# Half of the second feed-forward matrix by seven block products for eight, with the feed-forward stage ordered anew

## The reference

```python
f = rms_norm(h, g_ffn_pre[l])
f = jnp.square(jax.nn.relu(f @ w_ff1[l])) @ w_ff2[l]
h = h + rms_norm(f, g_ffn_post[l])
```

## Time and profile before

| | |
|---|---|
| median of 3 runs | 2151.79 us (2151.78 to 2152.73) |
| span of the profiled execution | 2150.6 us, 1.2 us under the median |
| PE busy | 2125.1 us (99%) |
| DVE busy | 1361.9 us (63%) |
| ACT busy | 1106.1 us (51%) |
| POOL busy | 156.2 us (7%), all in slices 21 to 25 of 40 |
| DMA | 395.17 MB, mean 184 GB/s |

### The profile page before, as it was taken

One profiled execution on the slowest core, in us unless ns is written; L12 is line 12 of the kernel. 1 busy time (PEld: TensorE's weight loads), 2 busy tenths in 40 slices (PEclk: granted clock), 3 DMA queues, 4 the chain that ended last, 5 costly groups with the idle time before them and its releaser, 6 DMA issues. The chain is left out here.

```text
span 2150.6 us, 29240 instructions
## 1 busy us (share of the span) xinstructions
PE 2125.1 (99%) x11602; PEld 1841.8 (86%) x11602; DVE 1361.9 (63%) x1979; ACT 1106.1 (51%) x1541; POOL 156.2 (7%) x78
## 2 busy tenths in 40 slices
PE   8999999999999999999999999999999999999998
PEld 7888888888988888888888888888888888888886
DVE  5554568875577558876578678766555555555555
ACT  4444554454464555555455455656435534544543
POOL 0000000000000000000007873000000000000000
PEclk9999999999999999999999999999999999999999
DMA  8666545655576655655656654646666666666664
GB/s 278 196 189 187 165 138 174 179 172 186 185 214 186 178 148 159 174 167 176 191 180 198 193 178 151 215 136 206 193 193 190 189 193 193 189 194 190 192 190 145
DMA packets 325031, 395.17 MB, mean 184 GB/s; under 512 B 20848, under 2 KB 252912, under 8 KB 324128
## 3 DMA queue, kind: packets, MB, share of 16 engines
q1 hardware_dynamic: 323104, 383.21, 59.0%
q0 software_dynamic: 1792, 10.10, 1.2%
HBM read 391.16 MB, written 2.10 MB: 183 GB/s over the span
## 5 line engine op out<-in xcount | busy, mean ns | idle before, releaser
L490 DVE TENSOR_TENSOR low<-raw,high 128x1024 fp32r<-128x1024 f32 (+2 forms) x672 | 809.9, 1209 | 639.0 <-ACT high L934 635.3
L934 ACT ACTIVATE high<-raw 128x1024 fp32r<-128x1024 f32 (+2 forms) x732 | 763.0, 1046 | 775.8 <-PE acc L682 201.7
L682 PE MATMUL acc<-xhl,high 128*128 128x512 f32 x3198 | 766.4, 391 | 0.0
L682 PEld LDWEIGHTS acc<-xhl,high 128*128 128x128 f32 x3198 | 587.0, 188 | 113.8 <-issue 0.7
L699 PE MATMUL acc<-xhl,low 128*128 128x256 f32 x3200 | 436.9, 286 | 1.9 <-DVE xhl L1792 1.4
L699 PEld LDWEIGHTS acc<-xhl,low 128*128 128x128 f32 x3200 | 414.4, 191 | 18.1 <-DVE xhl L1792 1.8
L686 PE MATMUL acc<-high,yhl 128*128 128x512 f32 (+1 forms) x1036 | 380.1, 373 | 2.2 <-DVE work L1718 1.6
L687 PE MATMUL acc<-high,yhl 128*128 128x512 f32 (+1 forms) x1036 | 378.8, 372 | 0.0
L702 PE MATMUL acc<-low,yhl 128*128 128x512 f32 (+1 forms) x1036 | 241.9, 374 | 0.2
L686 PEld LDWEIGHTS acc<-high,yhl 128*128 128x128 f32 x1036 | 195.2, 188 | 36.8 <-DVE work L1718 2.0
L687 PEld LDWEIGHTS acc<-high,yhl 128*128 128x128 f32 x1036 | 195.2, 188 | 33.8
(11 more groups left out here) (228 smaller groups left out, 1286.9 us busy)
## 6 DMA issues: line engine op xcount, KB each, us to landing
raw<-in_w_in SPq DMA_DIRECT2D x328, 512.0 KB, 3.7
raw<-in_w_ff SPq DMA_DIRECT2D x256, 512.0 KB, 3.9
raw<-in_w_out SPq DMA_DIRECT2D x91, 512.0 KB, 4.3
raw<-in_w_mem_kv SPq DMA_DIRECT2D x32, 512.0 KB, 5.0
raw<-in_w_in SPq DMA_DIRECT2D x16, 256.0 KB, 2.7
raw<-in_w_out SPq DMA_DIRECT2D x10, 256.0 KB, 2.8
x_nat<-in_mem SPq DMA_DIRECT2D x4, 512.0 KB, 7.8
x_nat<-in_x POOLq DMA_DIRECT2D x4, 512.0 KB, 6.4
```

The source lines that it names most:

```text
L490: eng.tensor_tensor(part(low, g), part(raw, g), part(high, g).bitcast(F32), ALU.subtract).then_inc(ready, 1)
L682: ins = pe.matmul(acc[:, 2 * (c.acc % 2) + s, :], wh[:, t, at], vhl, start=first, stop=last)
L934: act.activation(part(high, g), part(raw, g), ACT.Copy).then_inc(high_ready, 1)
```

## The change

The first matrix is now computed in 64 tiles of 128 hidden features (two blocks each, rows of 128 columns, 512 bytes of a row of the weights in one piece), apart from the first four, which stay in the old interleaved chunks. All tiles after tile 4 use one PSUM bank (`obank`). Two tiles are a pair: 256 hidden features.

The second matrix is cut in two. For the first 28 pairs, its columns 0 to 1023 are taken as 2 x 2 blocks of 128 hidden features by 512 columns, and the hidden features as 2 x 2 blocks of 128 rows by 128 features; Strassen's scheme (in Winograd's form) takes seven products of sums of blocks instead of eight. Such a *group* is 14 matmuls of 512 columns with high weight parts (`group_high`), one or two tiles, then 7 with low weight parts (`group_low`). The seven sums stay in seven PSUM banks over a run of four groups. After each run come eight *piece* blocks, the same four pairs by columns 1024 to 2047 in the plain way, and the products are added to SBUF. The last four pairs take plain pieces for all columns.

So ACT and DVE gain work: sums of weight blocks (`group_sums`), seven units of 512 columns to split instead of four, sums of hidden blocks (`pair_sums`) with eight units of 128 to split instead of four, copies of each tile out of its bank (`tile_copy`). The row norm is folded into the end (`epsv`), so the scaled sums `sq3` go. `low_part` writes the low part over the raw block, and a slot of `raw` is free only when PE has used it. The order on each engine is written out again; with p0 to p7 I call the eight piece blocks of a run. The accumulators in SBUF are set to zero by POOL.

The core of the diff (of PE, then ACT, DVE, SP):

```diff
+def ff_order():
+    yield from (("tile", 4), ("tile", 5))
+    for j in range(GROUPS):
+        yield ("high", j)
+        if BESIDE[j][0] is not None:
+            yield ("tile", BESIDE[j][0])
+        yield ("low", j)
+        yield ("tile", BESIDE[j][1])
+        if j % 4 == 3:
+            yield from (("piece", j // 4, n, i) for n in (2, 3) for i in range(4))
+    for i in range(2):
+        for n in range(2):
+            yield ("piece", RUNS, n, i)
+            yield ("tile", 60 + 2 * i + n)
+    yield from (("piece", RUNS, n, i) for i in (2, 3) for n in range(2))
+    yield from (("piece", RUNS, n, i) for n in (2, 3) for i in range(4))
...
             eng.wait_ge(high_ready, g + 1)
-            eng.tensor_tensor(part(low, g), part(raw, g), part(high, g).bitcast(F32), ALU.subtract).then_inc(ready, 1)
+            out = part(rawr if g >= FF1 else low, g)
...
+        def tile_bank(n):
+            return bank_of[1] if n == TILES_AHEAD else obank[:, :]
...
+            def feature_tile(n):
+                if n > TILES_AHEAD + 1:
+                    pe.wait_ge(tile_out, n - TILES_AHEAD)
+                    if n - 12 in range(0, 56, 8):
+                        pe.wait_ge(piece_out, 4 * ((n - 12) // 8) + 3)
...
+            def group_high(j):
+                pe.wait_ge(pair_ready, j + 1)
+                pe.wait_ge(split_high, 3 * j + 3)
+                for p, unit, n in PRODUCTS:
...
+            def group_low(j):
+                pe.wait_ge(split_low, 3 * j + 3)
+                for p, unit, n in PRODUCTS:
+                    ins = pe.matmul(bank_of[p], rows_of(0, j, n), bset_r[:, j % 2, unit, :], start=False, stop=j % 4 == 3)
+                ins.then_inc(group_used, 1)
...
+            def piece(e, n, i, rows=(0, 1)):
+                g, pair = by["f2", e, n].blocks[i], 4 * e + i
+                wh, wl = part(high, g), part(rawr, g)
+                banks = last_banks[n]
+                pe.wait_ge(pair_ready, pair + 1)
...
+            def x_squares(c):
+                act.wait_ge(norm_ready, norms(2, 2 * c + 1))
+                squares(x[:, :, CW * c:CW * c + CW], c, junk=ff_junk)
...
+            def tile_copy(n):
+                act.wait_ge(block_used, last_of(("g1", n)))
+                if n >= TILES_AHEAD + 2:
+                    act.wait_ge(pair_sq, n // 2)
+                act.activation(tcopy[:, n % 2, :], tile_bank(n), ACT.Copy).then_inc(tile_out, 1)
+            def relu_of(pair):
+                if pair < 2:
+                    act.wait_ge(folded, flip_no(by["f1", 0, pair]) + 1)
+                    v = cross
+                else:
+                    act.wait_ge(pair_fold, pair - 1)
+                    v = tcopy[:, :, 0:S]
+                act.activation(v, v, ACT.Relu).then_inc(pair_relu, 1)
+                act.wait_ge(pair_relu, pair + 1)
+                if pair:
+                    act.wait_ge(pair_ready, pair)
+                act.activation(combo[:, 0:4, :].rearrange("p (t s) n -> p t (s n)", t=2), v, ACT.Square).then_inc(pair_sq, 1)
...
+            def pair_h(pair):
+                if pair < 4 * RUNS:
+                    act.wait_ge(pair_step, 4 * (pair + 1))
...
+                if pair >= 6:
+                    act.wait_ge(block_used, last_of(("f2", (pair - 6) // 4, 3)))
...
+                    act.wait_ge(group_used, pair - 1)
+                act.activation(pair_units(0, pair), combos(pair), ACT.Copy).then_inc(pair_high, 1)
...
+            def ff_period(j):
+                n, b = next_blocks(j), BESIDE[j][0] is not None
+                p = {0: 2, 1: 3, 2: None, 3: 4}[j] if j < 4 else j + 1 if j % 4 else None
+                if j == 3:
+                    relu_of(p)
+                if j < 4 or j % 4:
+                    tile_copy(BESIDE[j - 1][1] if j else 5)
+                if b:
+                    round_block(n[2])
+                if j + 1 < GROUPS:
+                    split_h(j + 1, 0)
+                if p is not None and j != 3:
+                    relu_of(p)
+                if b:
+                    round_block(n[3])
+                if j + 1 < GROUPS:
+                    split_h(j + 1, 1)
+                    split_h(j + 1, 2)
+                if b:
+                    tile_copy(BESIDE[j][0])
+                if p is not None:
+                    pair_h(p)
+                m = n[4:6] if b else n[2:4]
+                round_block(m[0])
+                round_block(m[1])
...
+            def piece_run(e, g):
+                tile_copy(BESIDE[4 * e + 3][1])
+                round_block(g)
+                relu_of(4 * e + 5)
+                round_block(g + 1)
+                round_block(g + 2)
+                pair_h(4 * e + 5)
+                for b in range(3, 8):
+                    round_block(g + b)
...
+            cross_out(("f1", 0, 0))
+            round_block(FF1 + 2)
+            relu_of(0)
+            round_block(FF1 + 3)
+            cross_out(("f1", 0, 1))
+            split_h(0, 0)
+            pair_h(0)
+            split_h(0, 1)
+            split_h(0, 2)
+            round_block(FF1 + 4)
+            tile_copy(4)
+            relu_of(1)
+            round_block(FF1 + 5)
+            pair_h(1)
+            for c in range(4):
+                x_squares(c)
+            for j in range(GROUPS):
+                g = ff_period(j)
+                if j % 4 == 3:
+                    piece_run(j // 4, g)
+            g = BLOCKS - 24
+            for b, task in enumerate((None, None, None, None, None, 60, None, None, 61, 30, None, None, 62, None, None, 63)):
+                if b >= 2:
+                    round_block(g + b)
+                if task in (60, 61, 62, 63):
+                    tile_copy(task)
+                if task == 63:
+                    relu_of(31)
+                    pair_h(31)
+                if b == 9:
+                    relu_of(30)
+                if b == 10:
+                    pair_h(30)
...
+            def fold_pair(pair):
+                dve.wait_ge(tile_out, 2 * pair + 2 - TILES_AHEAD)
+                dve.tensor_tensor(tcopy[:, :, 0:S], tcopy[:, :, 0:S], tcopy[:, :, S:2 * S], ALU.add).then_inc(pair_fold, 1)
...
+            def pair_l(pair):
+                dve.wait_ge(pair_high, pair + 1)
+                dve.tensor_tensor(pair_units(1, pair), combos(pair), pair_units(0, pair).bitcast(F32),
+                                  ALU.subtract).then_inc(pair_ready, 1)
...
+            def group_sums(g):
+                units = bset[:, g % 2]
+                dve.wait_ge(group_landed[g % 2][0], 16 * (g // 2 + 1))
+                dve.tensor_tensor(units[:, 1, :], units[:, 1, :], units[:, 0, :], ALU.subtract).then_inc(sum_step, 1)
...
+            def pieces_out(e, n):
...
+            def ff_period(j):
+                n, b = next_blocks(j), BESIDE[j][0] is not None
+                p = {0: 2, 1: 3, 2: None, 3: 4}[j] if j < 4 else j + 1 if j % 4 else None
+                if j == 3:
+                    fold_pair(p)
+                if j + 1 < GROUPS:
+                    group_sums(j + 1)
+                if p is not None and j != 3:
+                    fold_pair(p)
+                if b:
+                    low_block(n[2])
+                if p is not None and p < 4 * RUNS:
+                    pair_sums(p)
+                if b:
+                    low_block(n[3])
+                if j + 1 < GROUPS:
+                    for part_no in range(3):
+                        split_l(j + 1, part_no)
+                if j % 4 == 3:
+                    sums_out(j // 4, OUTS[:3])
+                if p is not None:
+                    pair_l(p)
+                m = n[4:6] if b else n[2:4]
+                low_block(m[0])
+                low_block(m[1])
...
+            def piece_run(e, g):
+                p = 4 * e + 5
+                sums_out(e, OUTS[3:5])
+                low_block(g)
+                sums_out(e, OUTS[5:7])
+                fold_pair(p)
+                low_block(g + 1)
+                if p < 4 * RUNS:
+                    pair_sums(p)
+                low_block(g + 2)
+                pair_l(p)
+                low_block(g + 3)
+                pieces_out(e, 2)
...
+            fold(("f1", 0, 0))
+            low_block(FF1 + 2)
+            low_block(FF1 + 3)
+            fold(("f1", 0, 1))
+            pair_sums(0)
+            pair_l(0)
+            group_sums(0)
+            for part_no in range(3):
+                split_l(0, part_no)
+            low_block(FF1 + 4)
+            pair_sums(1)
+            low_block(FF1 + 5)
+            pair_l(1)
...
+            for b in range(2, 16):
+                low_block(g + b)
+                if b == 3:
+                    mix_sums()
+                if b == 9:
+                    fold_pair(30)
+                if b == 10:
+                    pair_l(30)
+            fold_pair(31)
+            pair_l(31)
...
+            def load_group(j):
+                if j < 2:
+                    sp.wait_ge(xt_ready, 40)
+                else:
```

(65 more changed lines are left out.)

377 lines of the change are left out of this document (266 added, 111 removed).

## The result

The changed kernel takes 2203.4 us (median of 4 runs, 2199.0 to 2205.7) against 2152.3 us (4 runs beside it, 2151.8 to 2153.3): ratio 1.0233, 95% interval 1.0219 to 1.0248, 51 us slower. The profiled execution is the fastest of the four: its span is 2197.2 us, 46.6 us longer than that of before. The forecast was 2166.7 us: slower was right, the size (14.4 us over the kernel before, for 51) was under a third of the real one.

What follows compares the result with a forecast made beforehand. PE's own pace was taken as the bound: -19.0 saved, +13.6 start, +11.8 p3, +8.0 end, +0.5 periods gave +14.9 us, a span of 2165.5 and a median of 2166.7 us; forecast 2156 to 2179, range 2150 to 2187.

Steps and rivals of the forecast that it cites:

- What bounds the kernel, what PE saves: Feed-forward stage: PE's own pace is the time; 21 matmuls for 24 in 28 groups save 19.0 us.
- Start: Stage start: PE waits 2.9 us before high 0, 8.9 before tile 6, plus 1.8 slow clock; 13.6 us.
- The squares' part: Start: ACT's eight squares stand ahead of tile 5's copy, which tile 6 needs; 5.9 us alone.
- Loads: Weight loads: 512 KB lands after 3.9 us, 1 MB 4.6, a block behind the group 4.4; short pieces 26 ns.
- A full period: Between groups: 15.9 us of PE, B's first block landing at 1.9; 0.5 us charged for all periods.
- It holds: Full period: ACT's copy of A and DVE's work are ready in time; 0.5 us charged, bounds 0 and 12.
- Rival (c): Period doesn't hold: A's copy or DVE late, 0.5 to 1 us in 24 periods; 2179 to 2191 us, chance 0.13.
- p3: Fourth piece of every run: PE waits for DVE's low part, 1.6 us six times and 2.2 once; 11.8 us.
- End: Last 24 blocks: tile 63 waits 3.0 us, tiles 61 and 62 0.3 each, pair 31 4.4; 8.0 us.
- The clock: Start, behind tile 6's wait: PE idles over 5.2 us, so its clock falls once; 1.8 us, bounds 0 and 3.
- At nothing: POOL's zeros, the seven mixing sums on DVE and the tail behind the last matmul add no time.
- The range: Range 2150 to 2187 us, leaving out (a), (d) and a small part of (b) and (c).

Runs made afterwards that it cites:

- the reordered run: Changed kernel with p3's rounding and low part put ahead of the pair's Relu and fold in the runs of pieces: 2186.4 us (1.0155).
- the four orders together: Changed kernel with squares later, p3 ahead of the pair, the end's order changed and tile A's copy earlier, all at once: 2157.5 us (1.0028).
- the last kernel: The 2151.4 us kernel with seven reorderings, plus four more changes aimed at single waits, one splitting the output's gain row load: 2144.3 us (0.9963).

## Why the prediction was right or wrong

The surplus of 31.7 us has two failed steps in it: the landings behind the group's load (12.1 us of longer waits in the middle) and the clock (9.6 us more than charged). The last chunk (2.4 us) and small terms make the rest. With half the group's load the time is 2180.6 us, in the range but still 14 over the forecast.

- **What bounds the kernel, what PE saves.** Right. Without waits a period is 15.9 us.
- **Start.** 13.6 forecast, 14.2 measured, each part within 0.8 us. The squares' part is shown by their removal. They were not all of it: behind them tile 7 waited, and the clock fell at high 0.
- **Loads.** This is the first step that failed. Pieces of 512 bytes took 28 ns each on average, packet by packet, for the 26 taken, so the price by the byte was right. What failed was "lands later: ... thus 4.4" (3.9 and 0.6 give 4.5) for the load behind the group: 6.1 was measured, and the group itself took 6.4 and 7.4 us. I took the group's 4.6 from a 1 MB load that had no stream of chunks around it. The trace of before has one in a stream, the 1 MB of `in_g_ffn_post` issued at 1379.9 us: it landed after 8.2 us, and two chunks' loads issued beside it after 8.0 and 8.2. The Trainium skill's fit (DMA: Bandwidth & Descriptors, Anatomy of one DMA) is for GpSimd's path and would have given an estimate of 4.4 for 1 MB; here, on SP's path, the trace disagrees, and with half the load the fit gives 3.2 where 4.8 was measured.
- **A full period.** "It holds" was wrong. Rival (c) had named the point, B's first chunk landing after 3.0 us; it lands at 3.7, and the true edge is 3.5. So (c)'s mechanism came with 0.2 to 1.3 us in 11 periods, not 0.5 to 1 in 24. It had 0.13 and was a matter of one landing time that I held at one value.
- **p3.** The place, the chain and its order were right, and shown by the reordered run. 11.8 became 17.1 (16.4 without p0's), within my bound of 18, by the same landing: with half the load it is 11.8.
- **End.** Tile 63 (3.0, measured 2.9) was right, pair 31 (4.4, measured 5.3) 0.9 short. Missed was the last chunk, 2.4 us; I had priced the later loads for the periods only and not for the place where chunks run in halves. The kernel before shows the same 2.1 us when it loads so.
- **The clock.** This is the second step that failed. Charged once, 1.8 us; in the stage it fell seven times and cost 11.4, mostly behind waits that were themselves forecast. I had taken from the earlier trace rows that PE must idle 5.2 us for it. That row showed an idle time after which it fell, not the shortest one. The cause is not only the late landings: with half the load, and the waits at their forecast size, it still fell five times.
- **At nothing.** Held, but for 0.6 us in the tail; in the profile with the squares moved the tail is 2.2 us longer than before, and why is open.
- **The range.** Its upper end, 2187, left out that landing, clock and last chunk could all go the same way. They did here. That a late landing brings more slow clock is shown in the middle (three falls, one with half the load); at the start and the end the clock fell with either landing.

## What to carry to other kernels

Where an engine takes its work in one fixed order, ask of each instruction what the next engine waits for behind it: here the order was worth 46 us on a change meant to save 19, and 59 with more reordering, low parts in other memory and a smaller load in one place. A transfer's time is to be taken from a row with the same traffic around it, and where a rival hangs on one landing, its chance is the chance of that landing. Give a wait of 2 us or more a chance of slow clock behind it: the same kernel shows such waits with it and without it.

## What the runs showed of the hardware

- The granted clock fell to 0.50 behind idle times of PE of 2.8 and 2.9 us (1641 and 1733 us of the changed kernel), behind one of 1.9 (1549 us with half the load) and, with the four orders together, behind one of 1.6 (2137 us, with one of 0.5 five us before it). It stayed at 1.00 behind others of 2.4 and 3.5 (1912 and 1475 us of the changed kernel) and, with the end reordered, of 2.95 (1641 us). The length of the idle time alone does not tell; what else does is open. A fall cost 1.4 to 2.9 us.
- Two loads of 512 KB issued 0.4 us apart in a stream of others landed after 6.4 and 7.4 us, one alone after 4.8. Rows of 2 KB instead of 4 KB took off 0.5. Why two take so much longer is open.
- The changed kernel's four runs differ by 6.7 us, the kernel before's beside them by 1.5. The load of the chunk behind a group lands after 4.6 to 7.4 us in one execution, which could make the difference, but that is not shown: the last kernel, with few waits left, still has 5.7 us between its six runs.
